# A router's chain with the gather in transposed form, and a last expert tile that ends by column halves

## The reference

```python
def moe_swiglu(h, router, w_in, w_out):
    logits = (hf @ router).astype(jnp.float32)          # 256 x 8
    top_v, top_i = lax.top_k(logits, TOP_K)             # 2 of 8
    top_w = jax.nn.softmax(top_v, axis=-1)
    ...
    for e in range(N_EXPERTS):
        y = y + gates[:, e:e + 1].astype(hf.dtype) * swiglu(hf, w_in[e], w_out[e])
...
x = x + g_f[:, None, :] * y
return rms_norm(x, final_norm)
```

## Time and profile before

| | us |
|---|---|
| median of 3 runs | 1599.66 (1599.07 to 1599.93) |
| profiled execution | 1597.54 |
| its span | 1595.8 |
| PE busy | 1527.4 (96%) |
| DVE busy | 1424.6 (89%) |
| ACT busy | 1070.8 (67%) |
| mean DMA rate | 314 GB/s |

### The profile page before, as it was taken

How to read it: one execution, slowest core, us unless ns; L and a number is a source line. 1 busy time by engine, 2 the same in 40 slices (tenths; PEclk the granted TensorE clock), 3 DMA queues, 4 the chain that set the end, 5 groups by cost and what they waited for, 6 DMA issues and landing times.

```text
span 1595.8 us, 22625 instructions
## 1 busy us (share of the span) xinstructions
PE 1527.4 (96%) x7203; PEld 1265.8 (79%) x7203; DVE 1424.6 (89%) x1644; ACT 1070.8 (67%) x1234; POOL 60.3 (4%) x47
## 2 busy tenths in 40 slices
PE   5999998999989998999999999999999999999996
PEld 5788876888869876788888888888888888888874
DVE  6989989778878766999999999999999999999995
ACT  3554445434447545788787888877888888887873
POOL 0222300000000110000000000000000000000000
PEclk9999999999999998999999999999999999999997
DMA  9977776888866332899999999999999999999991
GB/s 333 347 264 273 273 258 224 272 314 301 300 226 238 132 103 83 310 385 391 348 385 388 372 360 384 377 354 390 384 351 377 387 378 362 385 378 352 383 376 57
DMA packets 235121, 500.98 MB, mean 314 GB/s; under 512 B 9744, under 2 KB 40640, under 8 KB 235072
## 3 DMA queue, kind: packets, MB, share of 16 engines
q1 hardware_dynamic: 233904, 500.29, 86.1%
q10 hardware_dynamic: 1168, 0.07, 0.0%
HBM read 499.28 MB, written 1.05 MB: 314 GB/s over the span
## 4 chain that ended last, share of the span: by engine, by line
PE 76%; DVE 13%; DMA 4%; issue 4%; ACT 2%; SPq 0%; DVEq 0%; ACTq 0%
PE ps L531 21%; PE ps L533 21%; PE ps L532 21%; DVE w_lo L1639 4%; DMA ada<-in_ada_w 3%; DVE acc L1658 3%; PE ps L1053 1%; PE ps L1023 1%; PE ps L1024 1%; PE ps L815 1%; PE ps L817 1%; PE ps L819 1%; PE ps L1044 1%; PE ps L1046 1%; DMA raw<-in_ret_w_in 1%
## 5 line engine op out<-in xcount | busy, mean ns | idle before, releaser
L1639 DVE TENSOR_TENSOR w_lo<-raw,w_hi 128x1024 fp32r<-128x1024 f32 x834 | 986.0, 1228 | 53.3 <-ACT w_hi L1225 45.9
L1225 ACT ACTIVATE w_hi<-raw 128x1024 fp32r<-128x1024 f32 x834 | 850.7, 1056 | 196.8 <-PE ps L533 170.7
L531 PE MATMUL ps<-w_hi,RA 128*128 128x512 f32 x1360 | 542.2, 399 | 12.9 <-DVE w_lo L1639 5.2
L533 PE MATMUL ps<-w_hi,RA 128*128 128x512 f32 x1360 | 533.1, 392 | 0.0
L532 PE MATMUL ps<-w_lo,RA 128*128 128x512 f32 x1360 | 532.4, 391 | 0.0
L531 PEld LDWEIGHTS ps<-w_hi,RA 128*128 128x128 f32 x1360 | 257.2, 189 | 67.1 <-DVE w_lo L1639 6.7
L533 PEld LDWEIGHTS ps<-w_hi,RA 128*128 128x128 f32 x1360 | 257.0, 189 | 54.9
L532 PEld LDWEIGHTS ps<-w_lo,RA 128*128 128x128 f32 x1360 | 257.6, 189 | 51.9 <-issue 0.7
L531 PE MATMUL ps<-w_hi,hT_hi 128*128 128x512 f32 x400 | 160.6, 401 | 5.7 <-issue 4.0
L533 PE MATMUL ps<-w_hi,hT_lo 128*128 128x512 f32 x400 | 157.2, 393 | 0.0
L532 PE MATMUL ps<-w_lo,hT_hi 128*128 128x512 f32 x400 | 157.1, 393 | 0.0
(11 more groups left out here) (301 smaller groups left out, 1244.7 us busy)
## 6 DMA issues: line engine op xcount, KB each, us to landing
raw<-in_moe_w_in SPq DMA_DIRECT2D x224, 1024.0 KB
raw<-in_moe_w_out SPq DMA_DIRECT2D x112, 1024.0 KB
ada<-in_ada_w SPq DMA_DIRECT2D x46, 1024.0 KB, 7.3
raw<-in_ff_w_in SPq DMA_DIRECT2D x44, 512.0 KB
raw<-in_ret_w_in SPq DMA_DIRECT2D x16, 1024.0 KB
raw<-in_ff_w_out SPq DMA_DIRECT2D x11, 1024.0 KB
raw<-in_ret_w_in SPq DMA_DIRECT2D x16, 512.0 KB
raw<-in_ret_w_out SPq DMA_DIRECT2D x8, 1024.0 KB
```

The costliest lines, as they stand in the source:

```text
L531: pe.matmul(out, a_hi, b_hi, start=first, stop=False)
L533: return pe.matmul(out, a_lo, b_hi, start=False, stop=last)
L1225: act.activation(w_hi[:, cn % RING, cols], raw[:, cn % RAW, cols], ACT.Copy).then_inc(hi_done, 1)
L1639: v.tensor_tensor(w_lo[:, cn % RING, cols], raw[:, cn % RAW, cols], w_hi[:, cn % RING, cols].bitcast(f32), ALU.subtract).then_inc(lo_done, 1)
```

## The change

It has three parts.

1. *Choosing experts.* x of block 1 is made, counted and turned by column halves. Each block's choice of experts is one chain (`choose`), block 0's ahead of block 1's norm. The gate's broadcast is moved behind the router's second product, in two parts. `turn_over` and `run_up` go.
2. *First gather.* `gather_first` takes `hk_hi` and `hk_lo` as weights and `hot` as the moving side, so that the rows come out turned; `first_rows` scales and splits them by feature halves, half of it on each engine. Copy and transposes go. It stands ahead of the loop. Gates, expert order and loop entry stand behind it and behind the splits of the weights of the first two `up`.
3. *End.* The last weights are split inside the last step. The last `down`, gate, halves, scatter, sums and squares run by column halves.

```diff
             route(0)
             transpose_raw(1)
-            broadcast_gate(3, diag3, 2)
             route(1)
-            turn_over(0, 8)
+            broadcast_gate(3, diag3, 2, (0,))
...
+            def down_by_columns(c, m, n, p):
+                pe.wait_ge(eTl_ok, n + 1)
+                for k in range(2):
+                    for h in range(2):
...
+                            last = passes(ps[:, 4 + k, :], eT_hi[:, kc, :], eT_lo[:, kc, :], w_hi[:, s, cols],
+                                          w_lo[:, s, cols], False, kc == 3)
...
+                    if k == 0:
+                        last.then_inc(down_h, 1)
...
+            def gather_first(p):
+                ne = NL * p
+                pe.wait_ge(hot_ok, ne + 1)
+                for i in range(2):
+                    for c in range(4 * i, 4 * i + 4):
+                        out = ps[:, 6 - 2 * i + c // 2 % 2, (c % 2) * P:(c % 2 + 1) * P]
+                        for b in range(NB):
+                            pe.wait_ge(hk_ok, b + 1)
+                            pe.matmul(out, hk_hi[:, b, c * P:(c + 1) * P], hot[:, b, :], start=b == 0, stop=False)
+                            last = pe.matmul(out, hk_lo[:, b, c * P:(c + 1) * P], hot[:, b, :], start=False,
+                                             stop=b == NB - 1)
+                    last.then_inc(hgT_done if i else rows_done, 1)
...
-            pe.wait_ge(hk_ok, NB)
-            gather(0, 6)
+            gather_first(0)
             pe.wait_ge(npass_ok, 1)
...
-                turn_over(0, 4)
-                transpose_gathered(NL * p, 6)
-                run_up(0, hot[:, 0, :], hk_hi[:, 0, 0:TW], 7)
-                pe.wait_ge(hgl_ok, 2 * NL * p + 2)
-                up(U_MOE, m0, 0)
+                up(U_MOE, m0, 0, 2 * NL * p)
...
-                down(U_MOE + MOE_U - 2, me, me + (EU - 1), False, True)
-                scatter(ne)
+                down_by_columns(U_MOE + MOE_U - 2, me, me + (EU - 1), p)
+                scatter_by_columns(ne, p)
...
+            first_rows(0)
+            split(U_MOE + 3)
             gate_out(3, gate_f, 2)
-            split_quarters(U_MOE, 0, 3, 4)
             act.wait_ge(dm_ok, 1)
...
-                split(U_MOE + MOE_U - 2, me)
-                split(U_MOE + MOE_U - 1, me)
-                y_high(yg_ok, ne + 1, yh_ok)
+                act.wait_ge(yg_h, p + 1)
+                act.activation(y_hi[:, 0:TW], y32[:, 0:TW], ACT.Copy).then_inc(yh_h, 1)
+                act.wait_ge(yg_ok, ne + 1)
+                act.activation(y_hi[:, TW:D], y32[:, TW:D], ACT.Copy).then_inc(yh_ok, 1)
...
+                if n == 2 and b == 1:
+                    for k in range(2):
+                        cols = slice(k * TW, (k + 1) * TW)
+                        steps.link(v.tensor_tensor(tmp[:, b, cols], ps[:, 4 - 4 * k + b, :], gate[:, cols], ALU.mult))
+                        v.tensor_tensor(x[:, b, cols], x[:, b, cols], tmp[:, b, cols], ALU.add).then_inc(x_ok, 1)
+                    return
...
-                if j < EU - 1 or not last_one:
+                if j == EU - 1 and last_one:
+                    split_quarters(c, me, 12, 16)
+                else:
                     split_quarters(c, me, 13, 14)
...
+            first_rows(0, 0)
+            v.tensor_scalar(nil, ident[:, :], 0.0, None, ALU.mult).then_inc(nil_ok, 1)
+            split(U_MOE + 1)
+            split(U_MOE + 2)
+            split(U_MOE + 3)
+            dve.wait_ge(ex_ok, 1)
...
+            dve.wait_ge(ssh_ok, NB)
+            v.tensor_scalar(stat[:, 50:52], stat[:, 20:22], 1.0 / D, EPS, ALU.mult, ALU.add).then_inc(bias_ok, 1)
```

More of the change, by code:

```diff
@@ L590, in run_up, with broadcast_gate @@
                     pe.matmul(ps[:, bank, :], a, b, start=True, stop=True)
-            def broadcast_gate(g, dg, bank):
+            def broadcast_gate(g, dg, bank, parts=range(2)):
                 pe.wait_ge(diag_ok, g + 1)
-                for n in range(2):
+                for n in parts:
                     last = pe.matmul(ps[:, bank + n, :], ones[:, :],
                                      dg[:, 4 * n:4 * n + 4, :].rearrange("p c q -> p (c q)"), start=True, stop=True)
-                last.then_inc(gbc_done, 1)
+                if 1 in parts:
+                    last.then_inc(gbc_done, 1)
             pe.wait_ge(const_ok, 1)
@@ L1115, in scatter_few, with step @@
                 scatter_rows((2, 6), f_hotT, f_scat_done)
-            def step(j, me, ne, p, last_one=False):
+            def step(j, me, ne, p, later=None):
+                last_one = later is None and j > 1
                 c, n, unit, gone = U_MOE + 4 + RAW * (j - 1), me + j, j % EU, (j - 1) % EU
@@ L1494, in _, with first_rows @@
             split_quarters(U_MOE, 0, 2, 3)
+            raw_out(1)
             root_mean_square(3, 1)
-            raw_out(1)
+            split_quarters(U_MOE, 0, 3, 4)
             normed_high(1)
+            split_quarters(U_MOE, 0, 4, 6)
+            def first_rows(p):
+                ne = NL * p
+                for i in range(2):
+                    if i == 0:
+                        act.wait_ge(rows_done, p + 1)
+                    else:
+                        act.wait_ge(hgT_done, ne + 1)
+                    for c in range(4 * i, 4 * i + 2):
+                        ins = act.activation(hg32[:, c, :], ps[:, 6 - 2 * i, (c % 2) * P:(c % 2 + 1) * P], ACT.Identity,
+                                             bias=modc[:, FF1 + SH + c:FF1 + SH + c + 1], scale=scol[:, 4, c:c + 1])
+                    ins.then_inc(hg32a_ok if i else rows_a, 1)
+                    if i == 0:
+                        act.wait_ge(rows_a, p + 1)
+                        act.wait_ge(rows_b, p + 1)
+                    else:
+                        act.wait_ge(hg32a_ok, ne + 1)
+                        act.wait_ge(hg32b_ok, ne + 1)
+                    act.activation(hg_hi[:, 4 * i:4 * i + 4, :], hg32[:, 4 * i:4 * i + 4, :],
+                                   ACT.Copy).then_inc(hgh_ok, 1)
+            first_rows(0)
+            split(U_MOE + 3)
             gate_out(3, gate_f, 2)
-            split_quarters(U_MOE, 0, 3, 4)
             act.wait_ge(dm_ok, 1)
@@ L1599, in _ @@
                 with act.If(p):
-                    for h in range(2):
+                    for h in range(3):
                         split(U_MOE + h, m0)
-                gathered_out(NL * p, 6)
-                gathered_scaled(NL * p, 6)
-                gathered_high(NL * p)
-                split(U_MOE + 2, m0)
-                split(U_MOE + 3, m0)
+                    first_rows(p)
+                    split(U_MOE + 3, m0)
                 tile_silu(m0, U_MOE + 2, m0)
@@ L2022, in _, with choose @@
             mod_last(26)
+            def choose(b):
+                dve.wait_ge(rt_done, b + 1)
+                steps.link(v.scalar_tensor_tensor(logit[:, b, :], ps[:, 6 + b, 0:NE], stat[:, 6 + b:7 + b], sh_e, ALU.mult,
+                                                  ALU.add))
+                steps.link(v.max(mx[:, b, :], logit[:, b, :]))
+                steps.link(v.max_index(ridx[:, b, :], mx[:, b, :], logit[:, b, :]))
+                steps.link(v.tensor_copy(stat[:, 36 + 2 * b:38 + 2 * b], ridx[:, b, 0:2]))
+                for k2, oh in enumerate((oh1, oh2)):
+                    ins = v.tensor_scalar(oh[:, b, :], slot_no[:, 0:NE], stat[:, 36 + 2 * b + k2:37 + 2 * b + k2], None,
+                                          ALU.is_equal)
+                steps.link(ins)
+                v.tensor_tensor(sel[:, b, :], oh1[:, b, :], oh2[:, b, :], ALU.add).then_inc(sel_ok, 1)
             raw_out(0)
@@ new lines, in _ @@
+            for b in range(NB):
+                ins = v.tensor_scalar(gate_e[:, b, :], oh1[:, b, :], stat[:, 12 + b:13 + b], None, ALU.mult)
+            steps.link(ins)
+            for b in range(NB):
+                ins = v.scalar_tensor_tensor(gate_e[:, b, :], oh2[:, b, :], stat[:, 14 + b:15 + b], gate_e[:, b, :],
+                                             ALU.mult, ALU.add)
+            steps.link(ins)
+            steps.link(v.max_index(ridx[:, 0, :], order_n, counts_n))
+            steps.link(v.tensor_copy(stat[:, 17:18], ridx[:, 0, 0:1]))
```

196 lines of the change are left out of this document (123 added, 73 removed).

## The result

| | before | changed |
|---|---|---|
| median, four runs each | 1599.80 (1599.07 to 1600.42) | 1586.14 (1585.21 to 1587.33) |
| ratio | | 0.9915, 95% interval 0.9898 to 0.9932 |
| profiled execution, span | 1597.54, 1595.8 | 1586.83, 1585.1 |

The forecast was 1589.3 us, range 1584.0 to 1596.5. The change is faster, within the range, by 13.7 us in the medians. The two profiled executions differ by 10.7. What differs between the two measurements is not known; the gain of the medians is 7 to 14 us.

What follows compares the result with a forecast made beforehand. TensorE's expert stage was taken as a block of fixed length, so time is won only before and after it. 3.0 us (Parts 1 to 3) plus 7.4 (Parts 4 and 5) gave 10.4: median 1589.3 us, range 1584.0 to 1596.5.

Steps and rivals of the forecast that it cites:

- Part 1: Router, choosing experts: gather starts at 614.9 us, between 613.4 (clock up) and 615.6 (half clock), against 615.03 before.
- The half-clock case: Router's second product at half clock: takes 3.9 us, which takes back the 2.2 us gain; gather starts at 615.6.
- Part 2: First gather in transposed form: 32 narrow products at 0.19 us, 6.1 us in all, bounds 4.2 and 14.
- Part 3: Between gather and expert block: VectorE's 13.7 us queue sets the block's start at 637.0, 4.2 us before 641.19.
- The clock's charge: Start of the expert block: 1.2 us lost because TensorE's idle stretch of some 4 us drops the clock.
- Part 4: Last tile, last four splits moved earlier: 1.45 us from the earlier start and 2.0 us from the clock.
- The clock's share: Last tile's products: 2.8 us if the clock stays up, of which 70%, 2.0 us, was taken.
- Part 5: Kernel's end by column halves: 3.3 us from gate, halves, scatter and sums, 0.6 us from the norm.
- the router's part yields nothing: Rival at the router: longer VectorE stretch or dearer narrow products, only the end counts: 1592.3 us, chance 0.17.
- half clock in both places: Rival at router and end: gather at half clock, cold stretch behind it, gain 3.1 us: 1596.6 us, chance 0.08.
- the case with the clock up: Rival at router and end: full clock in both, end keeps all of its 8.2 us: 1585.0 us, chance 0.17.
- The slower case: Rival in the gather: narrow products at 0.98 us, 31 us for 32, whole 1613.5 us, chance 0.05.

Runs made afterwards that it cites:

- e9: The changed kernel run again, unaltered, on another chip: 1588.26 us, ratio 0.9951 to the kernel before.
- e4: Changed kernel with gates and expert order (with ScalarE's Exp) moved back ahead of the first scaled rows: 1585.51 us, ratio 0.9925.
- e3: Changed kernel with expert 0's rows gathered as before (8 wide products, copy, 8 transposes): 1589.65 us, ratio 0.9951.
- e6: Changed kernel with 24 needless products of 512 columns on TensorE in front of the first gather: 1592.94 us, one execution.
- e5: Changed kernel with two needless sums (2.4 us together) on VectorE behind its six low splits: 1589.09 us, one execution.
- e10: Changed kernel with the gate's broadcast back ahead of the router's second product, and gates and expert order back ahead of the first rows: 1584.73 us, ratio 0.9928.
- e7: Changed kernel with the gate's broadcast back between the transposes and the router's second product: 1588.09 us, one execution.
- e8: Kernel before with only the last four splits of weights moved ahead of the last tile's high and low half: 1595.84 us, one execution.
- e11: e10 with 9 needless wide products as fillers in TensorE's two gaps before the gather: 1583.31 us, ratio 0.9926.

## Why the prediction was right, and where it was off

**The total** came from parts that missed in both directions: 0.8 instead of 3.0 at the router, 8.4 instead of 7.4 at the end, 1.55 by a stretch that nothing changed. That the sum, 10.4 us, comes so near to the 10.7 of the profiles is luck in part. The 13.7 us of the medians likely overstate the change: on another chip (e9) it was 6.8 us, and by the distances it is 9.2.

**Part 1, start of the gather.** I took 12.6 us behind the gate product, between 11.1 with the clock up and 13.3 at half. It was 13.17 or 13.18 in four executions of the new form in this order with the early fall of the clock, and 11.5 and 11.7 in the two with the late one (e4, e3). So the two cases were right to 0.6 us, and no execution shows the 12.6 that I took between them; what I didn't see is that the clock in front of the router's product decides, and that it differs between executions whose instructions up to there are the same. The half-clock case takes the 2.2 us back, as I wrote (3.9 us for the product, measured 3.56): behind it the next instruction starts at 8.27 us, where before it was 8.50. Moved behind, the broadcast ran at half clock as well.

**Part 2, the gather.** The price of 0.19 was a mean over two clocks. Measured are 0.213 at half and 0.111 at full (e6), each somewhat under the transpose's 0.246 and 0.13, but the whole gather ran at half: 7.5 us with a first pair of 1.1, against 6.1. The Trainium skill (TensorE: Matmul & The Clock Gate, section "Wait — 56ns, not 53.3ns?") has 107 ns cold and 56 warm. The runs here show twice that for fp32r operands, 0.213 us in the changed kernel and 0.111 in e6, as the rows on transposes had spoken for.

**Part 3, VectorE as the bound.** Right in mechanism and size, with the early fall of the clock: 15.95 us from the end of the gather to the first transposes forecast, 15.83 measured, TensorE idle 3.1 where I said 4, and e5 shows that a delay there arrives whole. The clock's charge was 1.6, not 1.2. (The view behind the earlier trace rows has a second row that I left out, 1.1 us of waits for this same product, 0.85 of them at 641.19; it changes no term.) What I didn't ask is what the queue had been before: the gates and the expert order had stood where VectorE waits for the gather anyway (3.0 us idle in the changed kernel). Behind the gather they cost 1.1 (e10 against e7) to 1.7 us (e4), and in the changed kernel the clock besides.

**Part 4.** 1.4 us against 1.45. The clock's share was 2.9, all of it, not 70%: e8 shows it with the splits alone.

**Part 5.** Gate, halves, scatter and sums 3.4 us against 3.3, of which 0.4 is the scatter's clock (e8); the norm, from the last sum to the end of the span, 7.0 instead of 7.65, 0.65 against 0.6.

**The rivals.** At the router the yield lies between my forecast and "the router's part yields nothing", nearer to the latter. The mechanism there is that of "half clock in both places", a gather at half clock from 13.2 us on and a second cold stretch behind it, with a cheaper narrow product; at the end it is the case with the clock up. The slower case, a narrow product of 0.55 us or more, is out by a factor of 2.6.

## What to carry to other kernels

Before a step is moved out of a chain, look at what its engine does in that place: a vector step in front of a wait costs nothing there and its full length behind it, and wide products that bring the clock back can take as long as they save. Before the difference of two executions is put down to an edit, look whether the clock was alike ahead of the first edited instruction: here it was worth 1.7 us in the start and hid behind two of the edits. Where TensorE stops for a late engine, price the clock with the wait: at the end here it was twice the wait. Compare changes of under 1% by distances between instructions that both kernels have, since the stretch that nobody touched moved by more than the change.

## What I had not expected of the hardware

- A product of 128 columns in fp32r costs 0.111 us at full clock where one of 512 costs 0.23 (24 in 5.7 in the last tile): half the price for a quarter of the columns.
- The clock stayed at half for 20.5 us with TensorE busy 19.4 of them, through the router's product, the broadcast, the slots' products and the 32 narrow ones, and rose some 2.3 us after the wide expert products began at 621.42. In e11 it fell at about 611.5, with TensorE busy without a gap since 605.05 and five wide products done from 608.97 to about 610.3.
- Behind the last attention gate product the clock fell first after 2.4 to 2.8 us in nine executions, after 5.8 and 5.9 in two and after 9.2 in three. All three of the last have the broadcast in front of the router's product and both of the second have it behind; whether an execution is among the nine was settled before either ran.
- The same kernel reached its last attention gate product at 600.74 and at 602.78 us in two executions, and variants of it between 600.0 and 609.2, with no instruction changed up to there. From there to the end the same kernel took 984.36 and 984.32 us, both times with the early fall of the clock.
